# One raw turn instead of two ahead of the seven-product turns of each feed-forward block

## What is computed

```
def swiglu(h, w1, w3, w2):
    return (jax.nn.silu(h @ w1) * (h @ w3)) @ w2
```

## Time and profile before

| | us |
|---|---|
| median of three runs (2294.25 to 2295.7) | 2294.4 |
| the profiled execution, its own time | 2295.81 |
| its span on the core | 2294.0 |
| PE busy | 2236.3 (97%) |
| POOL busy | 1160.8 (51%) |
| DVE busy | 1123.5 (49%) |
| ACT busy | 1072.4 (47%) |
| mean granted TensorE clock | 0.993 |

### The profile page before, as it was taken

How to read it: one execution, slowest core, us unless ns; L and a number is a source line. 1 busy time by engine, 2 the same in 40 slices (tenths; PEclk the granted TensorE clock), 3 DMA queues, 4 the chain that set the end, 5 groups by cost and what they waited for, 6 DMA issues and landing times. The chain is left out here.

```text
span 2294.0 us, 35352 instructions
## 1 busy us (share of the span) xinstructions
PE 2236.3 (97%) x12536; PEld 1887.9 (82%) x12536; DVE 1123.5 (49%) x2070; ACT 1072.4 (47%) x2037; POOL 1160.8 (51%) x723
## 2 busy tenths in 40 slices
PE   7999999999999999999999999999999998999997
PEld 6999888777787789998878777677788877999986
DVE  4887524023441338884152788655511123787611
ACT  5555434245544555554333466644622235555433
POOL 3677558732272457774544522053344453676545
PEclk9999999999999999999999999999999999999999
DMA  4323334422221223323362211021123332233232
GB/s 173 103 99 110 94 96 151 120 74 70 69 92 56 65 93 110 104 97 101 93 155 77 83 38 47 10 83 56 46 92 93 99 101 65 92 109 110 90 93 93
DMA packets 81275, 206.59 MB, mean 90 GB/s; under 512 B 7440, under 2 KB 31120, under 8 KB 80912
## 3 DMA queue, kind: packets, MB, share of 16 engines
q1 hardware_dynamic: 72832, 191.92, 26.5%
q10 hardware_dynamic: 8336, 13.25, 2.0%
HBM read 199.71 MB, written 2.10 MB: 88 GB/s over the span
## 5 line engine op out<-in xcount | busy, mean ns | idle before, releaser
L672 POOL TENSOR_TENSOR parts<-slot,parts 128x512 fp32r<-128x512 f32 (+3 forms) x210 | 379.9, 1809 | 283.6 <-ACT parts L2263 281.8
L697 POOL TENSOR_TENSOR parts<-slot,parts 128x512 fp32r<-128x512 f32 x162 | 228.7, 1424 | 164.9 <-ACT parts L2319 162.5
L2263 ACT ACTIVATE parts<-slot 128x1024 fp32r<-128x1024 f32 (+2 forms) x173 | 157.2, 910 | 310.2 <-PE bank L906 266.0
L901 PE MATMUL bank<-hhi,parts 128*128 128x512 f32 x512 | 201.4, 393 | 4.2 <-POOL parts L672 4.2
L660 POOL TENSOR_TENSOR parts<-slot,lanes 128x1024 fp32r<-128x1024 f32 x42 | 81.3, 1936 | 237.2 <-PE bank L1801 115.9
L902 PE MATMUL bank<-hhi,parts 128*128 128x512 f32 x512 | 200.3, 391 | 0.0
L1063 PE MATMUL bank<-hhi,parts 128*128 128x256 f32 x756 | 188.7, 282 | 2.0 <-ACT sc L2363 2.0
L1064 PE MATMUL bank<-hhi,parts 128*128 128x256 f32 x756 | 189.0, 282 | 0.0
L669 POOL TENSOR_TENSOR parts<-slot,parts 128x512 fp32r<-128x512 f32 x55 | 71.2, 1295 | 220.2 <-ACT parts L2263 218.6
L1063 PEld LDWEIGHTS bank<-hhi,parts 128*128 128x128 f32 x756 | 144.1, 191 | 2.7 <-issue 2.5
L1064 PEld LDWEIGHTS bank<-hhi,parts 128*128 128x128 f32 x756 | 144.2, 191 | 0.1
(11 more groups left out here) (684 smaller groups left out, 6060.0 us busy)
## 6 DMA issues: line engine op xcount, KB each, us to landing
slot<-w SPq DMA_DIRECT2D x264, 512.0 KB, 3.6
slot<-w SPq DMA_DIRECT2D x88, 256.0 KB, 2.7
slot<-w SPq DMA_DIRECT2D x48, 448.0 KB, 3.2
hid<-w SPq DMA_DIRECT2D x8, 512.0 KB, 3.5
x<-xT ACTq DMA_DIRECT2D x4, 512.0 KB, 10.1
hid<-headtab ACTq DMA_DIRECT2D x8, 256.0 KB, 3.6
big<-cmpw ACTq DMA_DIRECT2D x4, 512.0 KB, 11.0
hid<-w SPq DMA_DIRECT2D x8, 256.0 KB, 2.6
```

The costliest lines, as they stand in the source:

```text
L672: pool.tensor_tensor(low, w, high.bitcast(F32), ALU.subtract).then_inc(splits, 1)
L697: pool.tensor_tensor(low, source, high.bitcast(F32), ALU.subtract).then_inc(splits, 1)
L901: pe.matmul(out, high[:, k, :], mhi[:, k, :], start=(start and k == 0), stop=False)
L2263: act.activation(parts[nth % 2][:, 0, 0:kt, :], slot[j][:, 0:kt, :], ACT.Copy).then_inc(highs, 1)
```

## The change

One of the two raw turns goes: each block has one raw turn, nine pair turns in the loop and the last one outside. SyncE, TensorE and GpSimd leave their part of the second raw turn out. TensorE writes panels 2 and 3 of the raw turn that is left into banks 4 and 5 instead of 0 and 1. ScalarE's order becomes: the fourth panel's high part, eight `gained` in a row, the first Silu, and then what stood behind the second raw turn. VectorE's becomes: first gate, `token_sum(0)` to `(2)`, `token_low(0)`, the first weight sum, `token_sum(3)`, `token_low(1)`, the sum's low part, `token_low(2)`, and only then the hidden tile 0, the second weight sum and the gating of tile 1. ScalarE and VectorE run nine pair turns as loops of four, four and one.

```diff
-EARLY = (4, 4)
+EARLY = (4, 4, 1)
-PAIRS = KF // 2 - 3
+PAIRS = KF // 2 - 2
-FFN_UP = dict(products=4, splits=4, highs=4, free0=2, free1=2, silus=2, gscaled=2)
-SECOND = dict(products=4, splits=4, highs=4, free0=1, free1=1, free4=1, free5=1, silus=2, gscaled=2)
+FFN_UP = dict(products=4, splits=4, highs=4, free0=1, free1=1, free4=1, free5=1, silus=2, gscaled=2)
...
# SyncE
-                    n.past(SECOND)
-                    for j in range(RING):
-                        sp.wait_ge(products, n.at("products", j + 1 - RING))
-                        sp.dma_start(slot[j][:, :, :], w8[panel[8] + 2 * RING + j]).then_inc(loaded[j], 16)
-                    panel[8] += 3 * RING
+                    panel[8] += 2 * RING
# GpSimd
-                for nth in range(4):
-                    split(nth, nth, "act")
-                n.past(SECOND)
# TensorE
-                emptied(0, 1)
-                h_panel(2, bank[0][:, :])
-                emptied(1, 1)
-                h_panel(3, bank[1][:, :])
-                n.past(FFN_UP)
-                for nth, b in enumerate((0, 1, 4, 5)):
+                for nth, b in ((2, 4), (3, 5)):
                     emptied(b)
                     h_panel(nth, bank[b][:, :])
-                n.past(SECOND)
+                n.past(FFN_UP)
# ScalarE, behind the copy of rinv
+                high_part(3, 3, 2)
+                for k in range(KD):
+                    gained(k, g)
                 raw_silu(0, 0, 1)
-                high_part(3, 3, 2)
-                for k in range(HK):
-                    gained(k, g)
-                high_part(4, 0, 3, load=2)
-                raw_silu(1, 0, 2)
-                high_part(5, 1, 4, load=2)
                 n.past(FFN_UP)
-                for k in range(HK, KD):
-                    gained(k, g)
-                high_part(2, 2, 1)
-                raw_silu(0, 0, 1)
-                high_part(3, 3, 2)
-                n.past(SECOND)
                 for a in range(3):
                     token_high(a)
# VectorE
                 raw_gate(0, 0, 1)
+                for a in range(3):
+                    token_sum(a)
+                token_low(0)
+                weight_sum_1(0, ahead=1)
+                token_sum(3)
+                token_low(1)
+                sum_low(4, 5, sum_bank[0][0])
+                token_low(2)
                 raw_hidden(0, 1, 0, 2, 1)
-                token_sum(0)
-                raw_gate(1, 0, 3)
-                raw_hidden(1, 1, 1, 4, 2)
-                n.past(FFN_UP)
-                for a in range(1, 4):
-                    token_sum(a)
-                raw_gate(0, 0, 1)
-                raw_hidden(0, 1, 2, 2, 1)
-                weight_sum_1(0, ahead=1)
-                for a in range(2):
-                    token_low(a)
-                sum_low(4, 5, sum_bank[0][0])
                 weight_sum_2(0, ahead=1)
                 raw_gate(1, 4, 3)
-                token_low(2)
-                raw_hidden(1, 5, 3, 4, 2)
-                n.past(SECOND)
+                raw_hidden(1, 5, 1, 4, 2)
+                n.past(FFN_UP)
                 sum_low(STEP_SLOT[0], 4, sum_bank[0][1])
                 token_low(3)
...
```

More of the change, by code:

```diff
@@ L3391, in ffn_up @@
                 for nth, turns in enumerate(EARLY):
-                    events = {**PAIR_TURN, **(dict(msteps=2) if loads else {}), **({} if nth else dict(hhis=1, hlos=1))}
+                    events = {**PAIR_TURN, **(dict(msteps=2) if loads and nth < 2 else {}), **({} if nth else dict(hhis=1, hlos=1))}
                     with n.turns(dve, turns, events) as i:
-                        pair_turn(i * 2 + (4 + 2 * done), squared=i + done if loads else None, early=None if nth else i)
+                        pair_turn(i * 2 + (2 + 2 * done), squared=i + done if loads and nth < 2 else None,
+                                  early=None if nth else i)
                     done += turns
@@ L3398, in ffn_up @@
                     n.past({"msteps": 1})
-                pair_turn(4 + 2 * done, True)
+                pair_turn(2 + 2 * done, True)
                 n.past(PAIR_REST)
```

## The result

The changed kernel takes 2319.47 us (median of four runs, 2318.86 to 2322.43), the kernel before beside it 2295.05 us: a ratio of 1.0103, 95% interval 1.0091 to 1.0115. It is 24.4 us slower, 4.0 more than the forecast 20.4. The profiled execution took 2319.2 us, its span is 2317.4 us, 23.4 over that of before.

A forecast was written before the change was run, and what follows sets the result against it. TensorE, busy 97% of a 2294.0 us span, was taken to bound the kernel. Cheaper turns -5.3, added idle time +20.5 and slower clock +5.2 gave +20.4 us, 2314.8 us, range 2304.0 to 2321.0.

The forecast's parts named there:

- The gain, 1.76 us a block: A raw turn of 21.76 us becomes a pair turn of 20.0: 5.3 us gained over three blocks.
- The chain: VectorE's work from R, the end of rinv's copy, sets the third quarter product: R + 22.8, 24.0, 23.2.
- the bare Silu of 0.7: Tile 1's Silu, before hidden behind token_low(2), stands bare between its gate and its raw_hidden: 0.7 us.
- the 0.35 us behind it: ScalarE's fourth token_high, seed and step_high end some 0.35 us behind tile 1's raw_hidden.
- GpSimd's share: Contention with GpSimd lengthens VectorE's token_low(2) by 1.4 us and raw_hidden by 1.0, 7.2 us over three blocks.
- Added idle time: TensorE's later start of the third quarter product behind panel 3: 4.8, 8.6 and 7.1 us, together 20.5.
- The clock's share: Granted clock falls behind TensorE's idle time before the third quarter product: 1.7 us a block, 5.2 in all.
- The cheaper chain: Rival: the clock stays up in most blocks or contention doesn't meet; +8 to +15 us, 2302 to 2310; chance 0.14.
- The costlier Silu: Rival: ScalarE's table load ahead of the first token_high moves the chain 1.4 us a block; +24.6, 2319.0; chance 0.05.
- The other side: Rival: the preparation stays hidden as before, only the cheaper turns count; -5.3 us, 2289.1; chance 0.04.
- One reason given against it: Against the other side: ScalarE's eighth gained copy can't be ready before R + 5 at any order.

The follow-up runs named there:

- e9: The changed kernel with 40 matmuls of 256 columns into an unused half bank between the second and third quarter product: 2313.7 us, ratio 1.0081.
- e4: The changed kernel with four of ScalarE's eight gained copies ahead of its root: 2313.8 us, ratio 1.0083.
- e1: The changed kernel with the old order: ScalarE's first Silu ahead of the fourth panel's high part, VectorE gating tile 0 before its token differences: 2307.3 us.
- e2: The changed kernel with GpSimd's first two low parts and difference on 8 of 128 columns, first pair turn's sums not the reference's: 2311.1 us.
- e5: The changed kernel's work reordered on VectorE and ScalarE to shorten the chain, tile 0 gated during the wait for gained copies: 2303.7 us, ratio 1.0034.
- e8: As e6, with ScalarE's copy of the second sum ahead of token_high(3) and VectorE's token_low(0) ahead of token_sum(2): 2295.0 us, ratio 0.9998.
- e6: As e5, with four gained copies ahead of ScalarE's root in blocks 2 and 3: 2299.9 us, ratio 1.0020.
- e3: The changed kernel with 24 matmuls of 256 columns into an unused half bank between the second and third quarter product: 2317.8 us, ratio 1.0099.

## Why the prediction was right

**The gain, 1.76 us a block.** Right: e9, whose clock stays up, has 197.5 to 197.6 us from the third quarter product to the end of the pair turns where the kernel before has 177.68, so one pair turn more is 19.9 us, against 20.0 in the sum, and it stands for a raw turn of 21.76. No idle time stands at the new loop boundary; the only one in these windows of the changed kernel is the 0.68 us in the last turn that was there before.

**The chain.** Forecast for the third quarter product R + 22.8, 24.0 and 23.2; it came at R + 23.1, 24.5 and 23.6. The row that ends TensorE's idle time, the waits for the gained copies, the bare Silu of 0.7 and the 0.35 us behind it stand in VectorE's timeline as they were worked out. Its parts were moved in experiments and moved the third quarter product: its start (e4), the gating's place and the bare Silu, not apart from each other (e1), GpSimd's share (e2, 2.65 us a block against my 2.4), the order as a whole (e5, e8). TensorE's idle time ahead of it is 5.1 us in blocks 1 and 3 as said, but 3.54 in block 2, under the 4 to 6 of the forecast: there 3.43 us stand ahead of the first quarter product instead.

**The terms that were mis-sized.** Added idle time 23.4 us against 20.5. The chain itself was short by 0.3 to 0.5 us a block, 1.2 us, of which GpSimd's share is 0.25 us a block. The other 1.6 is in block 1: I kept panel 2's slow 7.16 us of one execution as if it belonged to the kernel. Without it panel 3 ends earlier, and a chain that hangs on R gains nothing from that; the same 1.6 us are on the other side of the sum. The clock's share was 5.7 against 5.2, and that this came so near is partly luck. The 1.7 us a block were taken from the 0.76 of panel 2 behind 2.70 us of idle time; in the changed kernel the same 2.70 us at the same place were followed by a clock of 1.00, and the falls behind the 3.5 to 5.1 us cost 1.4 to 2.15. The remaining 1.2 us lie outside the blocks.

**The rivals.** The cheaper chain fell: the clock went down in all three blocks. The costlier Silu fell too, though its time, 2319.0, is close to what was measured; ScalarE in block 3 of the changed kernel:

```profile
1965.20 1.28 ACT L2301 ACT_TABLE_LOAD   x1
1966.49 0.63 ACT L2301 ACTIVATE silu<-ex 128x512 f32<-128x512 f32 x1
```

The Silu starts 0.01 us behind the load's end in its new place as well; a near number came from other terms. The Trainium skill, "ScalarE: Activation LUTs", section "What ACT_TABLE_LOAD costs", adds a drain of 1.38 us to a switch, by which the Silu would start 1.4 us later; the trace does not agree. The other side, -5.3 us, needed a chain shorter by 5 to 9 us. e8 shows that order and four moved copies make it 4.4, 8.5 and 7.6 us shorter, so the other side was nearly in reach, but the change's order went the other way. One reason given against it was wrong: the eighth gained copy can be ready before R + 5. With four of them ahead of the root it ends at R + 3.9 in block 3 of e4 (1960.42).

**What I left out.** I took the changed order as given and didn't ask what the old one would have given. The expectation of e1, worked out before that kernel was built, has it at about R + 21; it came at R + 21.25, 21.97 and 21.24. With that order the loss is about 12 us (e1).

## What to carry to other kernels

When work is taken away from the bounding engine, ask first what was made ready behind it: the gain was 5.3 us, and the cover that went with it held 14 us of another engine's work a block. Then write that engine's queue out as a chain to the instruction that the bounding engine waits for, and keep out of it everything that this instruction doesn't need; gating was moved to where it fell into a disturbed stretch, when its old place was an idle wait that cost nothing. Look for every small copy that somebody waits for before moving it: some 1.8 us of idle time a block came from one misplaced instruction of 0.38 us (e5).

## What the runs showed of the hardware that was not expected

The granted clock doesn't follow from the length of one idle time. TensorE's idle time of 2.70 us ahead of panel 2 of block 1 stands in eight of the traces. Behind it the clock fell to 0.50 in three (the kernel before, e5, e9) and stayed at 1.00 in five (the changed kernel, e1, e2, e6, e8). An idle time of 1.77 to 1.78 us ahead of the second quarter product was followed by 0.50 in block 1 of e6 and of e8, and by 1.00 in blocks 2 and 3 of e5. Behind 2.25 us it fell in two of two places (e3), behind the changed kernel's 3.54 to 5.13 us in three of three, and behind 0.34 to 0.48 us in none of three (e3, e9). Panel 2 takes 7.16 us in one outcome (the kernel before) and 5.54 in the other (the changed kernel), 1.6 us that a single trace can't tell from the effect of a change.

The price is more than the idle time's own: in e3 29 matmuls of 256 columns were issued in 5 us instead of 42, in the changed kernel 23. And filling the idle time with useless matmuls is worth something by itself: e9 is 5.7 us faster than the same kernel without them.
